# Seven block products in place of eight for gate, up and three quarters of down in the last stage of a three-stage f32 model

## What is computed

```python
        x = x + mix @ w_o[l]
        h2 = rmsnorm_3(x, norm2_w[l])
        f = (jax.nn.silu(h2 @ w_ffn_gate[l]) * (h2 @ w_ffn_up[l])) @ w_ffn_down[l]
        x = x + f
```

## Time and profile before

| | us |
|---|---|
| median of 3 runs | 2160.38 (2159.89 to 2164.29) |
| the profiled execution | 2160.32 |
| its span | 2158.4 |
| TensorE matmul busy | 2136.5 (99%) |
| TensorE weight load busy | 1825.7 |
| VectorE, ScalarE, GpSimd busy | 791.7, 376.5, 33.3 |
| mean granted clock of TensorE | 0.996 |

### The profile page before, as it was taken

How to read it: one execution, slowest core, us unless ns; L and a number is a source line. 1 busy time by engine, 2 the same in 40 slices (tenths; PEclk the granted TensorE clock), 3 DMA queues, 4 the chain that set the end, 5 groups by cost and what they waited for, 6 DMA issues and landing times.

```text
span 2158.4 us, 28385 instructions
## 1 busy us (share of the span) xinstructions
PE 2136.5 (99%) x9860; PEld 1825.7 (85%) x9860; DVE 791.7 (37%) x2198; ACT 376.5 (17%) x931; POOL 33.3 (2%) x52
## 2 busy tenths in 40 slices
PE   8999999999999999999999999999999999999998
PEld 6658788888888888888888888888888888888887
DVE  4133434953442355202982353165401034221100
ACT  2231421112111111110112112111101114110000
POOL 0000010000000000000000000000000000000000
PEclk9999999999999999999999999999999999999999
DMA  5304444333333444444433433444444432344443
GB/s 203 114 20 137 137 137 156 123 128 128 134 137 137 140 153 155 146 160 142 153 126 117 138 135 118 156 154 145 145 159 153 139 117 98 121 153 156 154 147 127
DMA packets 42257, 296.63 MB, mean 137 GB/s; under 512 B 4800, under 2 KB 4928, under 8 KB 8512
## 3 DMA queue, kind: packets, MB, share of 16 engines
q1 hardware_dynamic: 42176, 295.55, 40.0%
HBM read 294.48 MB, written 1.05 MB: 137 GB/s over the span
## 4 chain that ended last, share of the span: by engine, by line
PE 97%; DMA 1%; DVE 1%; ACT 0%; issue 0%; SPq 0%; ACTq 0%; DVEq 0%
PE bank L594 96%; DMA ring<-wstream 1%; PE bank L593 1%; DVE arena L1335 0%; DVE arena L1659 0%; DVE arena L1652 0%; ACT arena L995 0%; DVE tmp L1655 0%; ACT arena L1099 0%; ACT arena L1051 0%; DVE arena L1580 0%; DVE arena L1572 0%; ACT arena L1095 0%; ACT arena L1119 0%; DVE arena L1470 0%
## 5 line engine op out<-in xcount | busy, mean ns | idle before, releaser
L594 PE MATMUL bank<-xn,ring 128*128 128x256 f32 (+2 forms) x5216 | 1136.6, 380 | 0.4 <-DMA ring<-wstream 0.4
L594 PEld LDWEIGHTS bank<-xn,ring 128*128 128x128 f32 (+1 forms) x5216 | 988.4, 190 | 144.3 <-issue 3.7
L594 PE MATMUL bank<-arena,ring 128*128 128x256 f32 (+2 forms) x3368 | 747.3, 383 | 12.8 <-DMA ring<-wstream 10.7
L594 PEld LDWEIGHTS bank<-arena,ring 128*128 128x128 f32 x3368 | 639.8, 191 | 114.0 <-DMA ring<-wstream 12.7
L995 ACT ACTIVATE arena<-bank 128x256 f32<-128x256 f32 (+6 forms) x380 | 149.6, 397 | 1160.4 <-PE bank L594 974.6
L1335 DVE SCALAR_TENSOR_TENSOR arena<-arena,par (+2 forms) x712 | 299.8, 483 | 24.5 <-DVE arena L1891 3.2
L1335 DVE SCALAR_TENSOR_TENSOR x_res<-bank,x_res 128x256 f32<-128x256 f32 x48 | 20.4, 425 | 280.5 <-PE bank L594 280.5
L1335 DVE SCALAR_TENSOR_TENSOR arena<-arena,bank 128x256 f32<-128x256 f32 (+3 forms) x80 | 32.9, 423 | 201.1 <-ACT arena L995 185.2
L594 PE MATMUL bank<-arena 128*128 128x256 f32 (+9 forms) x448 | 94.7, 349 | 0.9 <-ACT arena L995 0.9
L594 PEld LDWEIGHTS bank<-arena 128*128 128x128 f32 (+5 forms) x448 | 62.5, 181 | 25.5 <-issue 15.9
L1018 ACT ACTIVATE arena<-x_res,par 128x256 f32<-128x256 f32 x40 | 20.3, 508 | 296.4 <-DVE x_res L1335 296.4
(11 more groups left out here) (168 smaller groups left out, 701.8 us busy)
## 6 DMA issues: line engine op xcount, KB each, us to landing
ring<-wstream SPq DMA_DIRECT2D x262, 1024.0 KB, 4.8
ring<-wstream SPq DMA_DIRECT2D x15, 768.0 KB, 4.1
cst<-consts SPq DMA_DIRECT2D x1, 2616.0 KB, 15.2
ring<-wstream SPq DMA_DIRECT2D x4, 512.0 KB, 3.7
h_res<-tokens SPq DMA_DIRECT2D x2, 544.0 KB, 5.5
out<-arena SPq DMA_DIRECT2D x1, 1024.0 KB, 4.1
ring<-wstream SPq DMA_DIRECT2D x2, 384.0 KB, 3.1
ring<-wstream SPq DMA_DIRECT2D x2, 288.0 KB, 2.7
```

The source lines that it names most:

```text
L594: return pe.matmul(o, lhs, rhs, start=start, stop=stop, skip_group_check=True)
```

## The change

The products of `C.up` and of three of the four column groups of `C.down` are made by Strassen's scheme in Winograd's form. A product of a weight block (2 halves of the rows by 2 tiles of columns) with the activations (2 halves of the rows by 2 halves of 128 tokens) needs 7 products of quarters in place of 8. The quarters of the weights are stored one behind the other (`quarters`), so a block has `n` pairs of row tiles, 4 in `C.up` and 4, 4, 3 in `C.down`.
- Sums of activations, four of them: once for all of `C.up` and once for each row group of `C.down` (`sum_acts`, on VectorE).
- Sums of weights, four for each block: two at once on VectorE (`mix`, one operation of `2n` tiles), and two in a row on GpSimd, into `mixed`, one buffer for each slot.
- TensorE (`fast_block`): seven products of `n` `mm` over 128 tokens; three into bank `x`, the four that need weight sums into bank `y`. The slot is released with the first of these four.
- ScalarE copies the first product to SBUF, and VectorE makes the four quarters of the output from it and the banks (`unite`, five operations); tanh and the gating then run on SBUF, 512 elements at a time.
- The fourth column group stays as it was (`C.down3`). The loops of TensorE, SyncE, VectorE and ScalarE over `C.up` are written out.

```diff
+
+def quarters(w, col, first, half):
+
+    tile = lambda k, c: w[P * k:P * k + P, c:c + P]
+    parts = [(0, col), (0, col + P), (half, col + P), (half, col)]
+    return np.concatenate([tile(k + dk, c) for dk, c in parts for k in first], 1)
...
     add("C.up", "w_ffn_gate_3+w_ffn_up_3", 0, its=10, n=2, size=2048,
-        part=lambda w, it, q: columns(w[q], span(256 * it + 256)))
-    add("C.down", "w_ffn_down_3", 0, its=2, n=6, size=None, part=down_part)
+        part=lambda w, it, q: quarters(w[q], 256 * it + 256, range(4), 4))
+    add("C.down", "w_ffn_down_3", 0, its=3, n=3, size=None, part=down_quarters)
+    add("C.down3", "w_ffn_down_3", 0, its=1, n=3, size=None, part=lambda w, it, q: down_part(w, 1, 3 + q))
...
+
+DOWN_PAIRS = (range(0, 4), range(4, 8), range(8, 11))
+
+
+def down_quarters(w, it, q):
+    return quarters(w, 256 * it, DOWN_PAIRS[q], 11)
...
+        mixed = [h_res[:, :, :].rearrange("p n t -> p (n t)")[:, 0:SLOT], area(1, SLOT)[:, 0, :]]
+        sum_up = area(4, 4 * P).rearrange("p s (k t) -> p s k t", t=P)
+        sum_down = arena[:, 24 * S:24 * S + 44 * P].rearrange("p (s k t) -> p s k t", s=4, t=P)
+        both, p1c = probs3[:, :, 0:S], decays3[:, :, 0:P]
+        partial = probt3[:, 0, 0:3 * P].rearrange("p (n t) -> p n t", t=P)
...
+        fast_blocks = [("C.up", it, q) for it in range(10) for q in range(2)] + \
+                      [("C.down", it, r) for it in range(3) for r in range(3)]
...
+                if stage in FAST:
+                    for i in range(kw["its"]):
+                        load(stage, i)
...
+            def fast_block(block, key, n, plain, sums, first=True, last=True, held=None, ready=None):
+
+                slot = e.next_block()
+                w = ring[:, slot, 0:4 * n * P].rearrange("p (s k c) -> p s k c", s=4, c=P)
+                m = mixed[slot][:, 0:4 * n * P].rearrange("p (s k c) -> p s k c", s=4, c=P)
+                banks = held or {}
...
+                def claim(half):
+                    if first:
+                        banks[half] = e.take("main", (key, half))
+                        pe.wait_ge(*e.emptied((key, half)))
...
+                def product(half, col, weight, act, opens=False):
+                    for k in range(n):
+                        ins = mm(banks[half], slice(0, P), slice(P * col, P * col + P), weight[:, k, :], act(k),
+                                 opens and first and k == 0, last and k == n - 1)
+                    return ins
+
+                pe.wait_ge(*e.landed(slot))
+                claim("x")
+                for event in ready or ():
+                    pe.wait_ge(*e.at(event))
+                product("x", 0, w[:, 0], lambda k: plain(0, k, 0), opens=True)
+                product("x", 2, w[:, 3], lambda k: plain(1, k, 0))
+                pe.wait_ge(*e.at((sums, "sum", 3)))
+                product("x", 1, w[:, 2], lambda k: acts_of(sums, 3, k)).then_inc(
+                    *e.done("main_done", ("pe", (key, "x")) if last else None))
+                claim("y")
+                pe.wait_ge(*e.at(("mixed", block)))
+                product("y", 1, m[:, 0], lambda k: acts_of(sums, 0, k), opens=True).then_inc(*e.done(f"slot_done{slot}"))
+                pe.wait_ge(*e.at((sums, "sum", 2)))
+                product("y", 2, m[:, 1], lambda k: acts_of(sums, 2, k))
+                product("y", 3, m[:, 2], lambda k: acts_of(sums, 1, k))
+                product("y", 0, m[:, 3], lambda k: plain(1, k, 1)).then_inc(
+                    *e.done("main_done", ("pe", (block, "t"))))
+                if last:
+                    e.counts.events["pe", (key, "y")] = e.counts.events["pe", (block, "t")]
+                return banks
...
-            blocks("C.up", 8, x256, S, ready=normed("C.n2"))
-            down_product("C.down", lambda k: hf3[:, k, :], S, [("C.hfj", 0), ("C.hfj", 1)])
+            for it in range(10):
+                for q in range(2):
+                    fast_block(("C.up", it, q), ("C.up", it, q), 4,
+                               lambda h, k, t: xn[:, 4 * h + k, P * t:P * t + P], "C.up",
+                               ready=normed("C.n2") if (it, q) == (0, 0) else None)
+            for it in range(3):
+                held = None
+                for r, ks in enumerate(DOWN_PAIRS):
+                    held = fast_block(("C.down", it, r), ("C.down", it), len(ks),
+                                      lambda h, k, t: hf3[:, 11 * h + ks[k], P * t:P * t + P], ("C.down", r),
+                                      first=r == 0, last=r == 2, held=held,
+                                      ready=[("C.hf", 10 if r == 2 else 7 + 2 * r)] if it == 0 else None)
+            held = None
+            for r, (k0, nk) in enumerate(down_rows):
+                held = halves("C.down3", 0, nk, [P, P], lambda k: hf3[:, k0 + k, :], S,
+                              first=r == 0, last=r == 2, held=held)
...
-            with e.turns("C.up", 10) as i:
-                for t in range(2):
-                    out_of(("C.up", 0, t), ft3[:, t, :], func=ACT.Tanh, scale=0.5, event=("C.ft", t), free=False)
+
+            def first_product(key, n):
+
+                act.wait_ge(*e.at(("pe", (key, "x"))))
+                b = e.bank_of((key, "x"))
+                act.activation(p1c[:, n % 2, :], psum[b][:, 0:P], ACT.Copy).then_inc(*e.step((key, "p1")))
+
+            for it in range(10):
+                for q in range(2):
+                    first_product(("C.up", it, q), q)
+                    if q == 0:
+                        for part in ("c11", "c12", "c22"):
+                            act.wait_ge(*e.at((("C.up", it, 0), part)))
+                        act.activation(ft3, fo3, ACT.Tanh, scale=0.5).then_inc(*e.step(("C.ft", it)))
+            for it in range(3):
+                first_product(("C.down", it), it)
...
+            for b in fast_blocks:
+                slot, turn = order[b]
+                size = pairs_of(b) * P
+                w, m = ring[:, slot, :], mixed[slot]
+                pool.wait_ge(sems[f"landed{slot}"], 16 * turn)
+                pool.wait_ge(*e.at(("mix1", b)))
+                pool.tensor_tensor(out=m[:, 2 * size:3 * size], in0=m[:, size:2 * size], in1=w[:, 0:size],
+                                   op=ALU.add).then_inc(*e.step(("mix2", b)))
+                pool.wait_ge(*e.at(("mix2", b)))
+                pool.tensor_tensor(out=m[:, 3 * size:4 * size], in0=w[:, 3 * size:4 * size],
+                                   in1=m[:, 2 * size:3 * size], op=ALU.subtract).then_inc(*e.done("combined", ("mixed", b)))
...
+            def unite(key, n, out, after=None):
+
+                if after:
+                    dve.wait_ge(*e.at(after))
+                x, y = psum[e.bank_of((key, "x"))], psum[e.bank_of((key, "y"))]
+                u2, u4, u3 = (partial[:, c, :] for c in range(3))
+                dve.wait_ge(*e.at((key, "p1")))
+                dve.tensor_tensor(out[:, 0, 0:P], x[:, 2 * P:3 * P], p1c[:, n % 2, :], ALU.add).then_inc(*e.step((key, "c11")))
+                dve.wait_ge(*e.at(("pe", (key, "y"))))
+                dve.tensor_tensor(u2, y[:, 3 * P:4 * P], p1c[:, n % 2, :], ALU.add).then_inc(*e.step((key, "u2")))
+                dve.wait_ge(*e.at((key, "u2")))
+                dve.tensor_tensor(partial[:, 1:3, :], y[:, P:3 * P].rearrange("p (n t) -> p n t", t=P),
+                                  partial[:, 0:1, :].broadcast_to([P, 2, P]), ALU.add).then_inc(*e.step((key, "u34")))
+                dve.wait_ge(*e.at((key, "u34")))
+                dve.tensor_tensor(out[:, 1, 0:P], x[:, P:2 * P], u4, ALU.add).then_inc(*e.frees((key, "x"), (key, "c12")))
+                dve.tensor_tensor(out[:, :, P:2 * P], y[:, 0:2 * P].rearrange("p (n t) -> p n t", t=P),
+                                  partial[:, 2:3, :].broadcast_to([P, 2, P]), ALU.add).then_inc(*e.frees((key, "y"), (key, "c22")))
+                dve.wait_ge(*e.at((key, "c12")))
+                dve.wait_ge(*e.at((key, "c22")))
+
...
+                if n >= len(fast_blocks):
+                    return
...
+                w, m = ring[:, slot, :], mixed[slot]
+                dve.wait_ge(sems[f"landed{slot}"], 16 * turn)
+                if n >= 2:
+                    dve.wait_ge(*e.at(("pe", (fast_blocks[n - 2], "t"))))
+                dve.tensor_tensor(m[:, 0:2 * size], w[:, size:3 * size], w[:, 0:2 * size], ALU.subtract).then_inc(*e.step(("mix1", b)))
+
+            def sum_acts(sums, a, lo, hi):
+
+                a11, a21, a12, a22 = a[:, lo, 0:P], a[:, lo, P:S], a[:, hi, 0:P], a[:, hi, P:S]
+                s1, s2, s3, s4 = ((sum_up[:, c] if sums == "C.up" else sum_down[:, c, lo]) for c in range(4))
+                dve.tensor_tensor(s1, a21, a22, ALU.add).then_inc(*e.step((sums, "sum", 0)))
+                dve.wait_ge(*e.at((sums, "sum", 0)))
+                dve.tensor_tensor(s2, s1, a11, ALU.subtract).then_inc(*e.step((sums, "sum", 1)))
+                dve.wait_ge(*e.at((sums, "sum", 1)))
```

(48 more changed lines are left out.)

26 lines of the change are left out of this document (24 added, 2 removed).

## The result

| kernel | median of runs, us | lowest to highest | span of the profiled run |
|---|---|---|---|
| before (four runs) | 2160.21 | 2159.89 to 2164.29 | 2158.4 |
| after (four runs) | 2145.97 | 2145.69 to 2146.63 | 2143.8 |

What follows compares the result with a forecast made beforehand. TensorE, busy for 2136.5 of 2158.4 us, was taken as the bound. Passes -18.7, first-block wait +3.9, clock +1.7, down +0.4 and extra waits +0.4 make -12.3 from 2160.32: 2148.0 us, range 2140 to 2157.

Steps and rivals of the forecast that it cites:

- Passes: TensorE in `C.up` and `C.down`: fewer matmul passes, 128-column ones at 0.1115 us, save 13.2 and 5.5, -18.7 us.
- The first block: Start of `C.up`: TensorE waits for serial sums on VectorE, then GpSimd; +3.9 us, ends 3.2 and 5.2.
- The clock: Behind the idle stretch at the start of `C.up`: granted clock may fall to 0.50; +1.7 us, ends 0 and 5.1.
- Steady state: Later blocks, one after another: loads and sums arrive in time with 1.9 us of spare; cost 0.
- Down's sums and the extra waits: Late mix behind `C.down`'s three-pair blocks, +0.4 us (ends 0, 2); more waits in TensorE's queue, +0.4 (ends 0, 2.9).
- The sum: Whole kernel: all terms together give -12.3 us against the profiled 2160.32, so 2148.0 us.
- the two small terms: Thin cover behind `C.down`'s three-pair blocks and more waits in TensorE's queue, +0.4 us each.
- GpSimd as the bound: Rival: GpSimd sums twice as long beside VectorE, 13.5 us where two blocks need 12.5; +14, 2162 us; chance 0.08.
- Does less than it says: Rival: a sum late in every block, from `unite` or a late load, 0.3 us each; +8.7, 2157 us; chance 0.06.

Runs made afterwards that it cites:

- split_before: The kernel before with each 256-column matmul in `C.up` cut into two of 128, no sums; 2165.03 us, ratio 1.0017 to the kernel before.
- fill: The changed kernel with eight needless 256-column matmuls on TensorE where it would wait in the first block; 2144.27 us, ratio 0.9928 to the kernel before.
- up_only: The changed kernel with `C.down` as in the kernel before, seven products only in `C.up`; 2152.06 us, ratio 0.9958 to the kernel before.
- double: The changed kernel with each of GpSimd's two weight sums per block made twice, same result; 2181.37 us, ratio 1.0106 to the kernel before.
- vector_sums: The changed kernel with GpSimd's two weight sums of every block given to VectorE; 2145.45 us, ratio 0.9928 to the kernel before.

## Why the prediction was right, step by step

- **Passes.** Forecast 0.1115 us each and -18.7 in sum. Measured 0.11165, -13.1 in `C.up` and -5.4 in down (462 x 0.11165 + 88 x 0.2158 against 352 x 0.2158), -18.5. Sixteen transposes in a row were enough of a sample: 1280 passes run at the pace that they showed, and `split_before` shows it without the rest of the change.
- **The first block.** Forecast +3.9, measured +3.4. The place, the releaser and the order of the operations were right. The term that was mis-sized is GpSimd's sum of 512 elements: 1.45 to 1.56 by the rows of 256 and 272, measured 1.27 and 1.32 here. From 256 to 512 it grows by 1.27 - 0.72 = 0.55 us, or 2.1 ns an element, so a fixed part of about 0.18 us was taken twice when I doubled 0.725; and the step from 256 to 272 (0.777 - 0.725, 3.3 ns an element) was no slope to extend over another 240. The estimate that the Trainium skill gave (GPSIMD Engine Reference, Elementwise — side-by-side cycle accounting), 1.1 us, is as far off to the other side.
- **The clock.** Forecast +1.7, measured +1.5, at the place that was named. `fill` shows that it is the idle time, and nothing that the new instructions do, that brings the clock down; `up_only` shows that the range up to 5.1 was needed, with 2.9.
- **Steady state.** Forecast no cost and 1.9 us of spare. In the timeline of after, TensorE needs the sums of one block at 2017.71 and GpSimd ends them at 2015.66, a spare of 2.05:

```profile
2011.35 1.23 DVE L2128 TENSOR_TENSOR arena<-ring 128x1024 f32<-128x1024 f32 x1 [0.97 <-DMA ring<-wstream]
2012.49 0.68 DVE L1467 SCALAR_TENSOR_TENSOR arena<-arena 128x512 f32<-128x512 f32 x1
2012.72 1.59 POOL L1451 TENSOR_TENSOR arena<-arena,ring 128x512 f32<-128x512 f32 x1 [2.88 <-DVE arena L2128]
2014.39 1.27 POOL L1454 TENSOR_TENSOR arena<-ring,arena 128x512 f32<-128x512 f32 x1
...
2017.71 1.06 PE L647 MATMUL bank<-arena 128*128 128x128 f32 x8
```

- **Down's sums and the extra waits.** Forecast +0.4 and +0.4, measured 0 and 0. Passes are 0.1117 apart across the waits as elsewhere. The tight block behind a three-pair one has its sums at 2083.90 and needs them at 2084.94, 1.0 us of spare where I had 0.2: its two sums take 0.5 us less than forecast, and the mix ends 0.3 earlier.
- **The sum.** Forecast -12.3, measured -14.6 in the span. Of the 2.3 between them 0.9 are the earlier start of `C.up`, which is chance; 0.6 the first wait and the clock, 5.0 together for 5.6; 0.8 the two small terms, less 0.2 in the passes. The last 0.2 lie in the trace of before: of the distances between its 352 passes of `C.down` four, at or next to the borders of the column groups, are 0.235 to 0.320 us long in place of 0.216. They have no cause that I can name. But for the pace, every term was taken on the dear side.
- **GpSimd as the bound.** Its chance of 0.08 stood on sums twice as long, and the changed kernel is not near it: a sum takes 1.59 at most in the steady state. `double` makes that rival true, and two blocks then take 13.74 us where the prediction has 13.5. That agreement is luck: the terms as written there add up to 13.3, and the slot's cycle, 13.27 without the hold, is not the one that binds. What binds is the chain of GpSimd's sums and a mix that can't overlap them, 6.88 us a block, which the prediction did not price although it named the exclusion. The price of +14 took the steady blocks alone; with the first block, the activation sums and the clock in it, `double` is 35 us over the changed kernel's median.
- **Does less than it says.** `unite` is never late. A late load happens: once in `fill`, 0.6 us; a 7.5 us landing is beyond what the 1.9 us of spare cover. In the trace of after there is none.

## What to carry to other kernels

Price a change of matmul shape by the distance of starts in the longest run of the new shape that the old trace has, never by the mean record, and then look for the one place where the new feeding work has no earlier block to hide behind: here the steady state cost nothing and one first block cost a quarter of the gain. A block there that is computed the old way gave back 3.5 of the 5 us, and nothing in the 19 others had to change. Count what the feeding engines share before splitting work between them: two sums on VectorE alone were quicker than the same two on GpSimd beside it.

## What the runs showed of the hardware that I had not expected

- GpSimd and VectorE hold each other up if VectorE's operation has two SBUF inputs: activation sums of 512 elements take 1.64 us beside GpSimd's sums and 0.69 alone, two scalar_tensor_tensor of 256 take 2.54 and 0.75, GpSimd's own sum 1.59 and 1.27. With a PSUM input there was no hold where this could be seen. The groups of after by form show both kinds, the held first sum and the free second:

```profile
L1451 POOL TENSOR_TENSOR arena<-arena,ring 128x512 f32<-128x512 f32 x13 | 19.7, 1514 | 67.5 <-DVE arena L2128 67.5
L1454 POOL TENSOR_TENSOR arena<-ring,arena 128x512 f32<-128x512 f32 x13 | 16.6, 1280 | 1.0
```

- The clock fell behind 1.9 us of idle time (`vector_sums`), and before it had stayed up behind 1.49. Behind the same 3.3 us it was low for 3.4 us in one trace (after) and for about twice that in another (`up_only`).
- A 1 MB load that mostly lands some 5 us after its issue was once waited for 7.5 us, with no other change nearby.
- An untouched part of the program ends up to 2.7 us apart between traces of kernels that share it, more than half of what the best repair here is worth (4.4).
